# Whole feature takes, four column quarters and one level step fewer in a two-block transformer kernel

## The chip, the cores and the metric

The kernel runs on one core of a Trainium2 chip. The metric is device time in microseconds of one execution. The kernel before was run three times: 1009.45, 1008.4 and 1008.05 us, median 1008.4. A fourth execution was profiled; the rows below come from it.

## The reference, cut to what matters

Two blocks follow each other on 256 tokens of 1024 features, in fp32.

```python
x = first_block(x, ...)       # attention with forget gates, sparse attention, then a 16-expert MoE
return second_block(x, ...)   # two layers:

def hybrid_layer(x, w_in, w_out, g_pre, g_post, lb, g_head, sinks):
    h = rms_norm_2(x, g_pre)
    proj = h @ w_in                                  # [256, 1024] x [1024, 6400]
    q_h, f_h, i_h, z_h, q_a, k_a, v_a, z_a = split(proj)
    o_h = hgrn2(q_h, f_h, i_h, lb)                   # gated recurrence over time, 8 heads of 128
    o_h = rms_norm_2(o_h, g_head) * silu(z_h)
    o_a = sliding_window_attention(rotary(q_a), rotary(k_a), v_a, sinks) * silu(z_a)
    y = concat([o_h, o_a]) @ w_out
    return x + rms_norm_2(y, g_post)
```

In `hgrn2` the query is silu(q_h), the forget gate f and the key 1 - f come from the sigmoid of f_h, and a score between two times is weighted, feature by feature, by the product of the f between them. In block 1 `compress_blocks` multiplies overlapping blocks of 32 tokens by a matrix of 2048 x 256, once for keys and once for values; there are 15 blocks for each of two groups.

## The kernel before, in words

TensorE (PE) multiplies fp32 numbers as fp32r, split in a high and a low part: high x high + high x low + low x high, three products for one (`mm3`, lines 599 to 601). ScalarE (ACT) makes the high part of each 128x512 piece of weights (`w_hi`, line 2027), VectorE (DVE) subtracts it from the raw piece and so makes the low part (`w_lo`, line 454, which is also the line of every other tensor_tensor). Line 457 is that of every tensor_scalar, line 604 that of every transpose by PE.

The work is cut into takes. A take uses two pieces of weights. The order on each engine is written by hand: every engine loops over the takes, feeds the weight pieces up to piece 2t + 9 (four and a half takes ahead), and does at each take what the table `beside` lists for it. A layer of block 2 has 66 takes. Takes 0 to 9 give the attention's q, k and v; takes 10 to 33 are feature takes, whose result has features on partitions and the 256 tokens on columns: za (8), then q, f, q, f (4 each); takes 34 to 49 give i and z of the recurrence by tokens; takes 50 to 65 are the output product. A feature take is 8 times three products of 256 columns (lines 599 to 601, called by `feature_take`); two takes share a PSUM bank, and ACT copies the bank after every second take. Sliding-window attention, eight jobs, runs between the feature takes, two takes apart from take 13 on: scores (line 766), the mask and the maxima on DVE, exponentials on ACT (line 2072), the division on DVE, transposes, `pt_buf` by ACT, values (line 796).

The recurrence is a tree of 8 levels (`level`, lines 1065 to 1087 on PE). At level 0 each time meets itself, at level 1 its neighbour, and so on to halves of 64. Each level is 32 small fp32 products (16 at the last), of 64 rows by 32 columns, which TensorE records as two matmuls each. Between the levels DVE multiplies Q and K by the decays (line 454, gates) and writes the scores through a mask into `buf_c` (line 1809). Levels stand behind takes 35, 37, ... 49. Before level 0, ACT makes sigmoid and silu of f and q (`qf_on`, lines 2102 to 2106), and DVE maps f and 1 - f into their bounds (`qf_bound`).

In block 1 the first matrix of `compress` is applied at takes 33 and 34 (line 820): 16 fp32 products each, of 64 columns of the array (two groups of 32 block slots) by 256 columns, keys to partitions 0 to 63 and values to 64 to 127.

GpSimd (POOL) does small powers, four memsets and the low parts of the experts' rows (line 2468).

Of the kernel before, what the change touches and what calls it, by code (L numbers as in the profile page):

```python
# [30 lines left out]
LEVELS = 8  # L31
AM_DVE, UPPER = 10, 5
# [55 lines left out]
LEVEL_AT = 35  # L88

OUT_L1, OUT_L2, TOK_L1, TOK_L2 = 14, 13, 6, 7  # L90
# [108 lines left out]
def beside_layer(l):  # L199
# [4 lines left out]
    for take, name, i in ((13, "za_on", 0), (20, "za_on", 1), (31, "qf_on", 0), (33, "qf_bound", 0), (33, "qf_on", 1),  # L204
                          (34, "qf_bound", 1), (44, "att_split", 0), (46, "att_split", 1)):
        table.setdefault(b + take, []).append((name, (l, i)))
    for lv in range(LEVELS):
        table.setdefault(b + LEVEL_AT + 2 * lv, []).append(("level", (l, lv)))
# [43 lines left out]
def build(nc, panels, x_in, prm_in, lay_in, pre_in, post_in, head_in, c1_in, c2_in, out):  # L252
    ctx = ExitStack()
    with ctx:
# [90 lines left out]
        blk = [buf_d[:, c * 1024:(c + 1) * 1024].rearrange("p (m g n) -> p m g n", m=16, g=2) for c in range(2)]  # L345
        kc_bd, vc_bd = buf_c[:, 1024:1088], buf_c[0:64, 1088:1216]
        Q, K, FG = gates[:, 0:2048], gates[:, 2048:4096], buf_d[:, :]
# [9 lines left out]
        def sem(name):  # L357
# [6 lines left out]
        w_hi_done = {"act": sem("w_hi_act"), "dve": sem("w_hi_dve")}  # L364
        w_lo_done = {"dve": sem("w_lo_dve"), "pool": sem("w_lo_pool")}
# [11 lines left out]
        forget_x, forget_l, forget, forget_b = (sem("forget_" + n) for n in ("x", "l", "f", "b"))  # L377
        bound_x, bound_e, bounds = sem("bound_x"), sem("bound_e"), sem("bounds")
        route_w, route_hi, route_lo = sem("route_w"), sem("route_hi"), sem("route_lo")
# [6 lines left out]
            sem("cmp_" + n) for n in ("mm", "v", "a", "z", "blk", "ms", "rs", "n", "s", "f"))  # L386
        up_hi, up_lo, mix, mix_hi, mix_lo = (sem(n) for n in ("up_hi", "up_lo", "mix", "mix_hi", "mix_lo"))
# [161 lines left out]

        def turns_of(x, lv):  # L550
            m = 1 << max(lv - 1, 0)
            return x.rearrange("p (b two m) -> p b two m", two=2, m=m)[:, :, 1 if lv else 0, :]
# [44 lines left out]
        def pe_program():  # L597
# [102 lines left out]

            def pair_turns(c, b, src3):
# [38 lines left out]
            def scores(job):  # L740
                pe.wait_ge(score_in, job)
                if job < FOX_JOBS:
                    pe.wait_ge(side, 5)
                    pe.wait_ge(forget_b, 1)
# [55 lines left out]
            def compress(step):  # L800
# [10 lines left out]
                elif step < 5:  # L811
# [6 lines left out]
                    for n in range(8):  # L818
                        for c in range(2):
                            m = T.matmul(ps[c * 64:(c + 1) * 64, 7, 0:256],  # L820
                                         blk[c][:, 8 * h + n, :, :].rearrange("p g n -> p (g n)"),
                                         w1[c][:, n, :], start=h == 0 and n == 0, stop=h == 1 and n == 7)
                elif step == 5:
                    pe.wait_ge(cmp_a, 1)
                    for i in range(2):
                        m = turn128(ps[:, 7, i * P:(i + 1) * P], scr[:, i * P:(i + 1) * P])
# [238 lines left out]
            def level(arg):  # L1065
                l, lv = arg
                b = 2 + lv % 2
                if lv == 0:
# [3 lines left out]
                else:  # L1072
                    pe.wait_ge(level_qk, LEVELS * l + lv)
                    if lv == LEVELS - 1:
                        pe.wait_ge(upper, UPPER * l + 1)
                    elif lv > 1:
                        pe.wait_ge(level_am, AM_DVE * l + 2 * (lv - 1))
                for n in range(NCH):
                    if lv == LEVELS - 1:
# [4 lines left out]
                    for h in range(2):  # L1084
                        c, half = n * P + h * HD, slice(h * HD, (h + 1) * HD)
                        m = T.matmul(ps[half, b, n * 32:(n + 1) * 32], K[:, c:c + HD], turns_of(Q[:, c:c + HD], lv),  # L1086
                                     start=True, stop=True)
                m.then_inc(level_mm, 1)

            def cross(arg):  # L1090
                l, j = arg
                pe.wait_ge(level_qk, LEVELS * (l + 1))
# [87 lines left out]
            for l in range(LAYERS):  # L1180
# [4 lines left out]
                for t in range(t0 + 4, t0 + L_ATT):  # L1185
# [5 lines left out]
                    elif r < L_IH:  # L1191
                        b, f = feature_at(t0 + L_ZA, t)
                        feature_take(t, b, f, 2 + l, uses + 3 + (r - L_ZA) // 4)
                    else:
                        token_take(t, (r - L_IH) % 4, PIECE, 1, 2 + l, uses + 9 + (r - L_IH) // 4)
# [13 lines left out]
        def dve_program():  # L1209
            fed = [0]  # L1210

            def feed(n):
                for p in pieces[fed[0]:n]:
                    if p.hi == "dve":
                        dve.wait_ge(*landed(p.load, p.part))
                        dve.wait_ge(taken, p.free)
                        V.tensor_copy(hi_of(p), raw_of(p)).then_inc(w_hi_done["dve"], 1)
                    if p.lo == "dve":
                        dve.wait_ge(w_hi_done[p.hi], p.hi_count)
                        tt(lo_of(p), raw_of(p), hi_of(p).bitcast(F32), ALU.subtract).then_inc(w_lo_done["dve"], 1)  # L1220
# [84 lines left out]
            def fox_k_(_):  # L1305
# [5 lines left out]
                V.tensor_copy(fsum, ps[:, 7, 0:S]).then_inc(forget_b, 1)  # L1311

            def lower(_):
# [12 lines left out]
                dve.wait_ge(route_hi, 1)  # L1326
                tt(wr3[:, :, 32:52], gw, wr3[:, :, 0:20].bitcast(F32), ALU.subtract).then_inc(route_lo, 1)
                dve.wait_ge(bound_e, 1)
# [144 lines left out]
            def compress(step):  # L1473
# [6 lines left out]
                elif step == 2:  # L1480
                    dve.wait_ge(cmp_v, 2)
                    dve.wait_ge(cmp_z, 2)
                    for c in range(2):
                        pos = prmc(("pos_k", "pos_v")[c])
                        for g in range(2):
# [4 lines left out]
                               ALU.add).then_inc(cmp_blk, 1)  # L1490
                elif step == 5:
                    dve.wait_ge(cmp_mm, 5)
                    V.tensor_copy(scr[:, 512:768], ps[:, 7, 0:256]).then_inc(cmp_v, 1)
# [266 lines left out]
            def qf_bound(arg):  # L1760
                l, j = arg
                dve.wait_ge(bounds, 3)
                for n, (buf, add) in enumerate(((FG, 8), (K, 16))):
                    dve.wait_ge(qf_sig, 6 * l + 4 * j + n + 1)
# [8 lines left out]
            def level(arg):  # L1773
                l, lv = arg
# [922 lines left out]
```

## Time and profile before

| | |
|---|---|
| median of 3 runs | 1008.4 us |
| profiled execution | 1006.5 us |
| its span, first to last instruction | 1004.5 us |
| granted TensorE clock, mean | 0.999 of 2.4 GHz |
| PE / DVE / ACT / POOL busy | 98% / 83% / 67% / 5% |
| HBM, mean | 209 GB/s |

The span is about 2 us shorter than the time of its execution, and that time about 2 us shorter than the median of the runs. "Busy" counts a matmul until its last result leaves the array, so that neighbours overlap; what a product costs is read from the distance between starts, not from its duration.

### The profile page before, as it was taken

How to read it: one execution, taken by the hardware profiler on the slowest of the kernel's cores; microseconds unless marked ns; L12 is line 12 of the kernel's file. 1: busy time of each engine (PE TensorE's matmuls, PEld its weight loads, DVE VectorE, ACT ScalarE, POOL GpSimd, SP SyncE). 2: the span in 40 equal slices, each digit the busy share in tenths (PEclk: the TensorE clock that was granted, in tenths of full speed). 3: DMA queues.
4: the chain of work that ended last, by engine and by line, in shares of the span. 5: the costliest groups of instructions: out<-in, count | busy, mean ns of one | idle time of the engine just before them, and what ended most of it. 6: DMA issues, size and time to landing. Idle time of an engine off the chain costs nothing.

```text
span 1004.5 us, 17322 instructions
## 1 busy us (share of the span) xinstructions
PE 983.4 (98%) x6553; PEld 839.8 (84%) x6553; DVE 834.1 (83%) x1609; ACT 668.3 (67%) x1339; POOL 51.5 (5%) x48
## 2 busy tenths in 40 slices
PE   8999999999999999999999999999999999999997
PEld 6878978987888888888878999888887999978885
DVE  6889867868999999999988777699578977689784
ACT  6475556547889889898865576836446477664552
POOL 1202000002002020020000000000100000000010
PEclk9999999999999999999999999999999999999999
DMA  8543253444999999999945343234454543333421
GB/s 349 217 168 126 88 230 145 147 185 158 384 395 340 403 365 355 411 341 385 388 171 200 146 153 143 88 128 164 147 209 153 183 147 127 127 127 127 169 85 42
DMA packets 32083, 211.34 MB, mean 210 GB/s; under 512 B 3584, under 2 KB 3584, under 8 KB 9216
## 3 DMA queue, kind: packets, MB, share of 16 engines
q1 hardware_dynamic: 30416, 204.22, 53.8%
q10 hardware_dynamic: 1584, 6.00, 1.7%
q8 instruction: 54, 0.88, 0.3%
q14 instruction: 29, 0.24, 0.1%
HBM read 209.16 MB, written 1.05 MB: 209 GB/s over the span
## 4 chain that ended last, share of the span: by engine, by line
PE 88%; DVE 7%; ACT 3%; issue 1%; POOL 1%; DVEq 0%; POOLq 0%; ACTq 0%
PE ps L599 25%; PE ps L601 24%; PE ps L600 23%; PE ps L604 4%; PE ps L1086 3%; PE ps L766 2%; DVE w_lo L454 2%; PE ps L796 2%; PE ps L820 1%; POOL stat L466 1%; PE ps L1140 1%; DVE gates L457 1%; DVE buf_d L457 1%; ACT op_rows L2027 0%; PE ps L1044 0%
## 5 line engine op out<-in xcount | busy, mean ns | idle before, releaser
L454 DVE TENSOR_TENSOR w_lo<-ring,w_hi 128x512 fp32r<-128x512 f32 (+1 forms) x624 | 392.9, 681 | 63.1 <-ACT w_hi L2027 61.0
L2027 ACT ACTIVATE w_hi<-ring 128x512 fp32r<-128x512 f32 (+1 forms) x624 | 354.9, 623 | 116.0 <-PE ps L601 108.6
L599 PE MATMUL ps<-w_hi,op_rows 128*128 128x512 f32 (+2 forms) x784 | 306.7, 391 | 6.3 <-DVE op_rows L1240 2.0
L601 PE MATMUL ps<-w_hi,op_rows 128*128 128x512 f32 (+2 forms) x784 | 300.9, 384 | 0.0
L600 PE MATMUL ps<-w_lo,op_rows 128*128 128x512 f32 (+2 forms) x784 | 300.5, 383 | 0.0
L599 PEld LDWEIGHTS ps<-w_hi,op_rows 128*128 128x128 f32 x784 | 147.3, 188 | 39.6 <-DVE w_lo L454 5.0
L601 PEld LDWEIGHTS ps<-w_hi,op_rows 128*128 128x128 f32 x784 | 147.3, 188 | 29.5
L600 PEld LDWEIGHTS ps<-w_lo,op_rows 128*128 128x128 f32 x784 | 147.5, 188 | 27.0
L599 PE MATMUL ps<-op_rows,w_hi 128*128 128x256 f32 x544 | 158.6, 291 | 0.0
L600 PE MATMUL ps<-op_rows,w_hi 128*128 128x256 f32 x544 | 153.8, 283 | 0.0
L601 PE MATMUL ps<-op_rows,w_lo 128*128 128x256 f32 x544 | 153.8, 283 | 0.0
L599 PEld LDWEIGHTS ps<-op_rows,w_hi 128*128 128x128 f32 x544 | 104.0, 191 | 3.8 <-issue 1.1
L600 PEld LDWEIGHTS ps<-op_rows,w_hi 128*128 128x128 f32 x544 | 104.1, 191 | 0.0
L601 PEld LDWEIGHTS ps<-op_rows,w_lo 128*128 128x128 f32 x544 | 104.0, 191 | 0.0
L2072 ACT ACTIVATE s_buf<-s_buf,stat 128x256 f32<-128x256 f32 (+1 forms) x112 | 49.6, 445 | 61.5 <-DVE stat L457 61.4
L466 POOL TENSOR_TENSOR stat<-stat,minus_half 128x1 f32<-128x1 f32 (+4 forms) x22 | 26.7, 1215 | 751.1 <-DVE stat L460 605.2
L454 DVE TENSOR_TENSOR w_lo<-two_ends,w_hi 128x512 fp32r<-128x512 f32 x64 | 43.5, 733 | 0.5 <-ACT w_hi L2027 0.5
L454 DVE TENSOR_TENSOR w_lo<-keys,w_hi 128x512 fp32r<-128x512 f32 x64 | 41.4, 700 | 0.4
L2027 ACT ACTIVATE w_hi<-two_ends 128x512 fp32r<-128x512 f32 x64 | 38.2, 624 | 4.6 <-PE ps L601 4.5
L2027 ACT ACTIVATE w_hi<-keys 128x512 fp32r<-128x512 f32 x64 | 37.8, 624 | 3.5 <-PE ps L601 3.5
L2027 ACT ACTIVATE zin<-ps 128x512 f32<-128x512 f32 (+2 forms) x32 | 17.7, 566 | 27.2 <-PE ps L1114 14.3
L1086 PEld LDWEIGHTS ps<-gates 128*64 128x64 f32 x896 | 27.3, 138 | 9.1 <-issue 9.1
(264 smaller groups left out, 1179.8 us busy)
## 6 DMA issues: line engine op xcount, KB each, us to landing
ring<-in_panels SPq DMA_DIRECT2D x161, 1024.0 KB, 5.0
keys<-in_panels SPq DMA_DIRECT2D x16, 1024.0 KB, 7.4
two_ends<-in_panels SPq DMA_DIRECT2D x16, 1024.0 KB, 7.7
cst<-in_c ACTq DMA_DIRECT2D x1, 1229.0 KB, 9.1
ring<-in_panels ACTq DMA_DIRECT2D x2, 512.0 KB, 5.8
buf_a<-in_pre ACTq DMA_DIRECT2D x2, 512.0 KB, 6.3
keys<-in_post ACTq DMA_DIRECT2D x2, 512.0 KB, 4.1
out<-head SPq DMA_DIRECT2D x2, 512.0 KB, 2.6
```

The lines of the kernel that those rows point to most:

```text
L454: return V.tensor_tensor(o, a, b, op)
L457: return V.tensor_scalar(o, a, s1, s2, op0, op1) if op1 is not None else V.tensor_scalar(o, a, s1, None, op0)
L466: return G.tensor_tensor(o, o, e.to_broadcast(list(o.shape)), ALU.pow)
L599: T.matmul(o, l[0], r[0], start=start, stop=False)
L600: T.matmul(o, l[0], r[1], start=False, stop=False)
L601: return T.matmul(o, l[1], r[0], start=False, stop=stop)
L604: return T.transpose(o, a, ident[0:n, 0:n])
L766: m = T.matmul(ps[:, 2 + e, lo:lo + n], q(a)[half, :], k[half, 0:n], start=True, stop=plain)
L796: m = T.matmul(value_of(job)[half, kt * P:S], v3[:, kt, cc:cc + HD], pt[:, kt * S:S + kt * P], start=kt == 0, stop=kt == 1)
L1086: m = T.matmul(ps[half, b, n * 32:(n + 1) * 32], K[:, c:c + HD], turns_of(Q[:, c:c + HD], lv), start=True, stop=True)
L2027: return A.activation(o, a, ACT.Copy, scale=scale)
L2072: i = A.activation(sc[:, lo:lo + n], sc[:, lo:lo + n], ACT.Exp, bias=ng_[:, c:c + 1], accum_out=sm[:, c:c + 1])
```

## The change

Six things change in the code.

1. A feature take becomes `whole_take`: for each of 8 feature tiles, one product of the high weights by 512 columns (high rows and low rows at once), and one of the low weights by 256. The halves of the sum lie in the two halves of a bank. Banks 0, 1 and 7 are used in turn; ACT copies the bank to a buffer after every take, GpSimd adds the halves.
2. The takes of f come before those of q. `keep_on` (sigmoids) stands at take 30, `q_on` (silu, written with pairs turned) at takes 32 and 33; the copy of a later take stands behind them on ACT.
3. Levels 1 and 2 become one step: products of 64 columns, 32 for each level. Seven steps stand behind takes 34, 36, 39, 41, 43, 45 and 47.
4. DVE's products of Q with the pairs' decays become `qf_pairs` and `scale_pairs`.
5. The zeroing of `buf_c` goes from DVE (take 4) to GpSimd (behind take 33).
6. `compress`: even and odd positions go to column quarters of 32 (slots of 16), ACT copies the odd half, DVE adds it. The rest (semaphores joined, unused feeding code of GpSimd gone) has no instruction of its own.

```diff
+LEVEL_AT = (34, 36, 39, 41, 43, 45, 47)
+FEATURES, FEATURE_BANKS = 24, (0, 1, 7)
...
+            def whole_take(l, t, i, n, uses):
+                w = weights_of(t)
+                b = FEATURE_BANKS[i % 3]
+                if i > 2:
+                    pe.wait_ge(feature_mid, FEATURES * l + i - 2)
...
+                for k in range(KT):
+                    rows_ready(n, k, 1)
+                    c = k % 4 * P
+                    hi, lo = (x[:, c:c + P] for x in w[k // 4])
+                    if k:
+                        T.matmul(ps[:, b, 0:S], lo, hi3[:, k, :], start=False, stop=False)
+                    m = T.matmul(ps[:, b, :], hi, op_both[:, :, k, :], start=k == 0, stop=k == KT - 1)
+                    if k == 0:
+                        T.matmul(ps[:, b, 0:S], lo, hi3[:, k, :], start=False, stop=False)
+                m.then_inc(taken, 1)
...
+                        if r == L_IH:
+                            pe.wait_ge(feature_mid, FEATURES * (l + 1))
...
+                    elif L_ZA <= r < L_IH:
+                        i = r - L_ZA
                         act.wait_ge(taken, t + 1)
-                        copy((Q if n < 4 else K)[:, c:c + 512], ps[:, b, :]).then_inc(out_free[b], 1)
+                        if i > 3:
+                            act.wait_ge(feature_out, FEATURES * l + i - 3)
+                        copy(feature_tmp(i), ps[:, FEATURE_BANKS[i % 3], :]).then_inc(feature_mid, 1)
...
+            def feature_sum(l, t, i):
+                n = i % 8
+                pool.wait_ge(swa_T, 5 * l + 4)
+                pool.wait_ge(feature_mid, FEATURES * l + i + 1)
+                y = feature_tmp(i)
+                G.tensor_tensor((za, K, q_raw)[i // 8][:, n * S:(n + 1) * S], y[:, 0:S], y[:, S:2 * S],
+                                ALU.add).then_inc(feature_out, 1)
...
+            def q_on(arg):
+                l, j = arg
+                act.wait_ge(feature_out, FEATURES * l + 20 + 4 * j)
+                act.wait_ge(value_mm, L1_JOBS + SWA_PAIRS * (l + 1))
...
+            def scale_pairs(hi):
+                was, now, f4 = (x.rearrange("p (b f) -> p b f", f=4) for x in (q_turned, Q, FG))
+                p2 = pairs_f.rearrange("p (b two) -> p b two", two=2)
+                dv(tt(now[:, :, 2 * hi], was[:, :, hi], f4[:, :, 2 * hi], ALU.mult))
+                dv(tt(now[:, :, 2 * hi + 1], was[:, :, 2 + hi], p2[:, :, hi], ALU.mult))
...
+                        if step == 1:
+                            m = T.matmul(ps[half, 2 + n // 8, n % 8 * HD:(n % 8 + 1) * HD], K[:, c:c + HD],
+                                         q_two[:, :, c:c + HD].rearrange("p y (b f) -> p y b f", f=4)[:, :, :, 2:4],
+                                         start=True, stop=True)
...
+                    for n in range(4):
+                        for q in range(4):
+                            odd, c = divmod(q, 2)
+                            m = T.matmul(ps[q * 32:(q + 1) * 32, 7, 0:256],
+                                         blk[c][:, 8 * h + 2 * n + odd, :, :].rearrange("p g n -> p (g n)"),
+                                         w1[c][:, 2 * n + odd, :], start=h == 0 and n == 0, stop=h == 1 and n == 3)
```

PE at the end of the feature takes of a layer, before: the last feature tile of take 33 and the first weight piece of take 34 (`op_rows` are the rows of the layer's input, high or low).

```order
L599 MATMUL ps<-op_rows,w_hi 128x256
L600 MATMUL ps<-op_rows,w_hi 128x256
L601 MATMUL ps<-op_rows,w_lo 128x256
L599 MATMUL ps<-w_hi,op_rows 128x512
L600 MATMUL ps<-w_lo,op_rows 128x512
L601 MATMUL ps<-w_hi,op_rows 128x512
```

The same place now.

```order
L729 MATMUL ps<-op_rows,w_lo 128x256
L730 MATMUL ps<-op_rows,w_hi 128x512
L613 MATMUL ps<-w_hi,op_rows 128x512
L614 MATMUL ps<-w_lo,op_rows 128x512
L615 MATMUL ps<-w_hi,op_rows 128x512
```

A feature tile of three products of 256 columns has become one of 256 and one of 512. The token takes (lines 613 to 615) are as before, but the first of them now stands behind a wait for the copy of take 33.

ACT before, from the weights of take 30 on: `pt_buf` are the copies of the last two attention jobs, `gates<-ps` the copies of takes 31 and 33, `buf_d` and `gates<-gates` sigmoid and silu.

```order
L2027 ACTIVATE pt_buf<-ps 128x768
L2027 ACTIVATE w_hi<-ring 128x512 x2
L2027 ACTIVATE pt_buf<-ps 128x768
L2027 ACTIVATE gates<-ps 128x512
L2103 ACT_TABLE_LOAD
L2103 ACTIVATE buf_d<-gates 128x1024
L2104 ACTIVATE gates<-gates 128x1024
L2106 ACT_TABLE_LOAD
L2106 ACTIVATE gates<-gates 128x1024
L2027 ACTIVATE w_hi<-ring 128x512 x4
L2027 ACTIVATE gates<-ps 128x512
```

ACT now, from the copy of take 30 (`buf_c<-ps`) to the table load before silu.

```order
L2094 ACTIVATE buf_c<-ps 128x512
L2165 ACT_TABLE_LOAD
L2165 ACTIVATE buf_d<-gates 128x1024
L2166 ACTIVATE gates<-gates 128x1024
L2165 ACTIVATE buf_d<-gates 128x1024
L2166 ACTIVATE gates<-gates 128x1024
L2094 ACTIVATE w_hi<-ring 128x512 x2
L2094 ACTIVATE pt_buf<-ps 128x768
L2094 ACTIVATE buf_c<-ps 128x512
L2094 ACTIVATE w_hi<-ring 128x512 x2
L2094 ACTIVATE buf_c<-ps 128x512
L2173 ACT_TABLE_LOAD
```

ACT now, the rows that follow; the last `buf_c<-ps` is the copy of take 33, for which PE waits before take 34.

```order
L2173 ACTIVATE q_two<-gates 128x256x2x2
L2094 ACTIVATE w_hi<-ring 128x512 x2
L2094 ACTIVATE buf_c<-ps 128x512
L2173 ACTIVATE q_two<-gates 128x256x2x2
L2094 ACTIVATE w_hi<-ring 128x512 x8
```

All four sigmoids now stand ahead of three copies, and one table load is gone from the stretch.

DVE before, from the weights of loop 35 to the masks of level 2; `gates<-gates,buf_d` is the product of Q or K with the decays, COPY_PREDICATED a level's masks.

```order
L454 TENSOR_TENSOR w_lo<-ring,w_hi 128x512 x4
L454 TENSOR_TENSOR gates<-gates,buf_d 128x1024
L1809 COPY_PREDICATED buf_c<-cst,ps 64x16x32 x2
L454 TENSOR_TENSOR w_lo<-ring,w_hi 128x512 x4
L454 TENSOR_TENSOR buf_d<-buf_d 128x1024
L454 TENSOR_TENSOR gates<-gates,buf_d 128x2048
L1809 COPY_PREDICATED buf_c<-cst,ps 64x16x32 x2
L454 TENSOR_TENSOR w_lo<-ring,w_hi 128x512 x4
L454 TENSOR_TENSOR gates<-gates,buf_d 128x512x2 x2
L454 TENSOR_TENSOR buf_b<-buf_d 128x512
L1809 COPY_PREDICATED buf_c<-cst,ps 64x16x16x2 x2
```

DVE now, from the second half of `scale_pairs` to the masks of steps 0 and 1 and the weights behind them.

```order
L462 TENSOR_TENSOR q_two<-q_two,buf_d 128x512
L462 TENSOR_TENSOR q_two<-q_two,pt_buf 128x512
L1843 COPY_PREDICATED buf_c<-cst,ps 64x16x32 x2
L462 TENSOR_TENSOR w_lo<-ring,w_hi 128x512 x4
L462 TENSOR_TENSOR q_two<-q_two,pt_buf 128x512x2
L462 TENSOR_TENSOR gates<-gates,pt_buf 128x512x2
L462 TENSOR_TENSOR buf_b<-pt_buf 128x512
L1843 COPY_PREDICATED buf_c<-cst,ps 64x16x32 x2
L1843 COPY_PREDICATED buf_c<-cst,ps 64x16x16x2 x2
L462 TENSOR_TENSOR w_lo<-ring,w_hi 128x512 x6
```

Four masks, those of levels 1 and 2, now stand in one piece ahead of the weights, where two masks stood between each two takes' weights; `qf_pairs` (a 128x1024 product to `pt_buf`) and the first half of `scale_pairs` stand ahead of this piece.

## Rows read from the trace of the kernel before

**Rows 1.** Part 1 of the page: busy time, share, instructions.

```profile
PE 983.4 (98%) x6553; PEld 839.8 (84%) x6553; DVE 834.1 (83%) x1609; ACT 668.3 (67%) x1339; POOL 51.5 (5%) x48
```

**Rows 2.** Waits of PE: total us, times, longest us.

```profile
PE ps L1086 <- DVE gates L457: 4.0, 2, 2.0
```

**Rows 3.** Timeline of PE: start us, duration; products of 512, then 256 columns.

```profile
535.73 0.39 PE L601 MATMUL ps<-w_hi,op_rows 128*128 128x512 f32 x1
...
545.93 0.39 PE L601 MATMUL ps<-w_hi,op_rows 128*128 128x512 f32 x1
...
547.27 0.28 PE L601 MATMUL ps<-w_hi,op_rows 128*128 128x256 f32 x1
...
550.15 0.28 PE L601 MATMUL ps<-w_hi,op_rows 128*128 128x256 f32 x1
```

**Rows 4.** Chain that ended last: start us, us on the chain.

```profile
668.50 0.43 PE ps L599
...
697.10 1.99 PE ps L1086 x64
...
704.75 1.08 PE ps L1081 x32
...
785.42 0.87 PE ps L604 x8
```

**Rows 5.** Timeline of PE: the compress product.

```profile
144.02 3.67 PE L820 MATMUL ps<-ring,buf_d 128*64 128x256 f32 x32
```

**Rows 6.** Timeline of PE, layer 0: behind take 30, and start of take 33.

```profile
631.25 0.87 PE L796 MATMUL ps<-pt_buf,zin 128*64 128x256 f32 x8
...
640.06 0.39 PE L599 MATMUL ps<-op_rows,w_hi 128*128 128x256 f32 x1
```

**Rows 7.** Timeline of ACT, layer 0, takes 30 to 33.

```profile
630.68 0.80 ACT L2027 ACTIVATE pt_buf<-ps 128x768 f32<-128x768 f32 x1
...
635.84 0.60 ACT L2027 ACTIVATE gates<-ps 128x512 f32<-128x512 f32 x1 [2.06 <-PE ps L601]
636.46 1.28 ACT L2103 ACT_TABLE_LOAD   x1
637.75 1.06 ACT L2103 ACTIVATE buf_d<-gates 128x1024 f32<-128x1024 f32 x1
638.72 1.04 ACT L2104 ACTIVATE gates<-gates 128x1024 f32<-128x1024 f32 x1
...
642.03 2.19 ACT L2027 ACTIVATE w_hi<-ring 128x512 fp32r<-128x512 f32 x4
```

**Rows 8.** Timeline of POOL: beside an almost idle DVE, then a busy one.

```profile
242.37 0.74 POOL L2468 TENSOR_TENSOR op_rows<-gates,op_rows 128x256 fp32r<-128x256 f32 x1 [1.81 <-ACT op_rows L2027]
...
302.12 3.60 POOL L2468 TENSOR_TENSOR op_rows<-gates,op_rows 128x256 fp32r<-128x256 f32 x2 [57.39 <-ACT op_rows L2027]
```

**Rows 9.** Timeline of DVE: without, then beside POOL's two adds after 306 us.

```profile
298.86 2.49 DVE L454 TENSOR_TENSOR w_lo<-ring,w_hi 128x512 fp32r<-128x512 f32 x4
...
306.20 3.59 DVE L454 TENSOR_TENSOR w_lo<-two_ends,w_hi 128x512 fp32r<-128x512 f32 x4
```

**Rows 10.** Timeline of DVE, layer 0, bounds and levels.

```profile
647.68 0.74 DVE L454 TENSOR_TENSOR zin<-ps,scr 128x256 f32<-128x256 f32 x2
648.35 1.37 DVE L457 TENSOR_SCALAR buf_d<-buf_d,lay 128x256 f32<-128x256 f32 x4
...
664.50 2.67 DVE L1809 COPY_PREDICATED buf_c<-cst,ps 64x512 f32<-64x512 uint32 x2
...
669.62 2.36 DVE L454 TENSOR_TENSOR gates<-gates,buf_d 128x1024 f32<-128x1024 f32 x2
671.89 1.08 DVE L454 TENSOR_TENSOR buf_b<-buf_d 128x512 f32<-128x512 f32 x1
```

**Rows 11.** Busy time by stage: attention, levels (PE, PEld, DVE, ACT, POOL; clock, DMA, GB/s).

```profile
580.00:610.00 30.00, 30.00 (x257) 27.99 (x255) 23.08 (x58) 22.30 (x54) 0.00 (x0) 1.00 0.41 153
651.20:705.00 53.80, 53.80 (x626) 44.90 (x628) 50.55 (x64) 26.15 (x48) 0.00 (x0) 1.00 0.41 147
```

**Rows 12.** Line of the attention's scores: durations ns, first and last start.

```profile
L766 PE MATMUL ps<-keys,zin x64: 269/324/480, 565.5 to 624.5; 64*128 64x256 f32 x32, 64*128 64x128 f32 x32
```

More of the change, by code:

```diff
@@ L203, in beside_layer @@
     at_takes(table, [(j0 + i, tuple(b + take for take in takes)) for i, takes in enumerate(ATT_2)])
-    for take, name, i in ((13, "za_on", 0), (20, "za_on", 1), (31, "qf_on", 0), (33, "qf_bound", 0), (33, "qf_on", 1),
-                          (34, "qf_bound", 1), (44, "att_split", 0), (46, "att_split", 1)):
+    for take, name, i in ((13, "za_on", 0), (20, "za_on", 1), (30, "keep_on", 0), (30, "keep_on", 1), (32, "q_on", 0), (33, "q_on", 1),
+                          (32, "qf_bound", 0), (33, "qf_bound", 1), (34, "qf_pairs", 0), (44, "att_split", 0), (46, "att_split", 1)):
         table.setdefault(b + take, []).append((name, (l, i)))
-    for lv in range(LEVELS):
-        table.setdefault(b + LEVEL_AT + 2 * lv, []).append(("level", (l, lv)))
+    for step, take in enumerate(LEVEL_AT):
+        table.setdefault(b + take, []).append(("level", (l, step)))
     for j in range(2):
@@ L548, in k_of, with feature_tmp, bank_of @@
             return K[:, j * 1024:(j + 1) * 1024]
+        def feature_tmp(i):
+            return buf_c[:, i % 4 * 512:(i % 4 + 1) * 512]
+        def bank_of(step):
+            return 7 if step in (0, 2) else 2 + (step + 1) % 2
         def turns_of(x, lv):
@@ new lines, in level @@
+            def level(arg):
+                l, step = arg
+                lv = step + 1
+                if step == 0:
+                    f2, k2 = (x.rearrange("p (b two) -> p b two", two=2) for x in (FG, K))
+                    dve.wait_ge(qf_sig, 6 * (l + 1))
+                    settle()
+                    scale_pairs(1)
+                    dve.wait_ge(level_mm, STEPS * l + 1)
+                    settle()
+                    tt(k2[:, :, 0], k2[:, :, 0], f2[:, :, 1], ALU.mult).then_inc(level_qk, 1)
+                    scale_pairs(0)
+                    dve.wait_ge(am_zero, l + 1)
+                    take_masked(l, 0, ps[:, bank_of(0), :].rearrange("p (n x) -> p n x", n=NCH), 0)
+                    return
+                dve.wait_ge(level_mm, STEPS * l + step + 1)
+                m = 1 << step
+                tot = pairs_f if step == 1 else buf_b[:, slice(*totals[lv - 1])]
+                qv, kv = (x.rearrange("p (b two m) -> p b two m", two=2, m=m) for x in (Q, K))
+                tv = tot.rearrange("p (b two) -> p b two", two=2)
+                dve.wait_ge(level_qk, STEPS * l + step)
+                settle()
+                tt(qv[:, :, 1, :], qv[:, :, 1, :], bc(tv[:, :, 0], m), ALU.mult)
+                last = tt(kv[:, :, 0, :], kv[:, :, 0, :], bc(tv[:, :, 1], m), ALU.mult)
+                if step + 1 < STEPS:
+                    last = tt(buf_b[:, slice(*totals[lv])], tv[:, :, 0], tv[:, :, 1], ALU.mult)
+                last.then_inc(level_qk, 1)
+                if step == 1:
+                    both = ps[:, 2:4, :].rearrange("p a (n y x) -> p (a n) y x", y=2, x=32)
+                    take_masked(l, 1, both[:, :, 0, :], 2)
+                    take_masked(l, 2, both[:, :, 1, :], 4)
+                elif step < 4:
+                    take_masked(l, lv, ps[:, bank_of(step), :].rearrange("p (n x) -> p n x", n=NCH), 2 * lv)
@@ L1911, in behind @@
                 for name, arg in beside.get(t, ()):
-                    if name in table and name not in ("log_in", "weigh", "scores_out", "qf_bound", "up_split"):
+                    if name in table and name not in ("log_in", "weigh", "scores_out", "qf_bound", "qf_pairs", "up_split"):
                         table[name](arg)
@@ L1992, in dve_program @@
                     ahead(t)
-                    if r == 4:
-                        V.memset(buf_c[:, :], 0.0).then_inc(am_zero, 1)
                     behind(t)
```

227 lines of the change are left out of this document (101 added, 126 removed).

## The prediction

> **What bounds the kernel now.** I read the busy times first. The reader is to see PE busy for 98% of the span and DVE, the next, for 83% [rows 1]. Next come PE's waits: of all that compete, one line concerns the edited stages, level 0's first product waiting for DVE's bound gates, 4.0 us in two waits, one a layer [rows 2]. So in these stages PE sets the pace, and a shorter PE program is a shorter kernel, unless another engine is late instead. How near the others are is read in busy time by stage: in 30 us of attention DVE is busy for 23.08 and ACT for 22.30, in the levels DVE is busy for 50.55 of 53.8 [rows 11]. The attention stage has room for new work on DVE and ACT; the level stage has almost none on DVE. Last I read PE's timeline for prices by spacing, since durations overlap: a run of 512-column products goes from 535.73 to 545.93 in 45 steps, 0.2267 each, one of 256-column products from 547.27 to 550.15 in 24 steps, 0.12 each [rows 3].
>
> **Feature takes.** A feature tile goes from three products of 256 columns (3 x 0.12 = 0.36) to one of 512 and one of 256 (0.2267 + 0.12 = 0.3467). Eight tiles a take: 2.88 becomes 2.77, 0.107 saved. With 24 takes and two layers, 48 x 0.107 = 5.1 us, 2.55 a layer. What is saved is the fixed part of a product; the columns streamed are the same.
>
> **Levels.** One step of 32 products goes: 1.99 on the chain, and the restart of the 512-column products behind it, where the first stands 0.43 on the chain instead of 0.23, so 0.2 [rows 3, 4]. The merged step has 64-column products; 64 records of 32 columns take 1.99, 32 records of 64 columns 1.08 [rows 4], so I put it at 2.15 for 1.99. Net -2.05 a layer.
>
> **Compress.** The 32 records of 256 columns come in 3.67 us, 0.115 each [rows 5]. A single fp32 stream would need more: transposes of 128 columns take 0.87/8 = 0.109 each [rows 4], about twice that for a record of 256. So the two column halves run beside each other. If four quarters do the same, each of the two multiplications halves; 3.67 includes some 0.2 of the last record's own end, so 2 x 3.45/2 = -3.45; if only two run at a time, nothing. I take the first, since a quarter differs from a half by the same division of columns and the halves show no loss. The Trainium skill (TensorEngine Tiling (Array Packing), Tiling Modes) lists 128x32 as four independent tiles, which would give the -3.45; no row here shows four. The added ACT copy and DVE add of the odd half stand one take ahead of the use, in a stage where PE alone is full; I cost them at nothing, and uncovered they would cost about 1 us each time, by a 0.60 copy [rows 7] and 0.74 for two sums of 256 columns [rows 10].
>
> **The new wait before take 34.** Level 0's wait goes: 2.0. PE now waits before take 34 for ACT's copy of take 33. Take t = 0 at 631.25, the values product behind take 30. Take 33 began 8.81 later [rows 6]; two shorter takes make it 8.6, and its end 11.4. ACT in its new order, each step at its pitch (about 0.1 under the duration; the sigmoids follow each other by 0.97) [rows 7]: 0.2 until the bank is full, copy 0.6, table 1.3, four sigmoids 3.9, two high parts 1.05, `pt_buf` 0.7, copy 0.5, two high parts 1.05, copy 0.5, table 1.3, silu 1.0, two high parts 1.05, copy of take 33 0.6: 13.75. PE waits 2.4. Queued behind that copy on ACT are the second silu and the high parts of later takes, which are four takes ahead and not late. POOL's add (0.74 alone [rows 8]) and the last silu end at 15.7, behind a take 34 that runs from 13.8 to 16.5, so level 0 itself is not late. Nothing is bound on SP: the weights' transfers are issued from there as before. The zeroing of `buf_c` stands behind the last add on POOL and before the first mask, near 24.
>
> **DVE in the level stretch.** ACT's last sigmoid ends at 6.0; behind it and the low parts due by then DVE works without a pause from about 7.7, an estimate: three values of 0.35, sixteen bounds 5.2, two pairs of low parts 2.4, `qf_pairs` 1.2 (17.55), a pair of low parts 1.2, `scale_pairs` 2 x 1.08, K 1.2 (22.1), `scale_pairs` 2.15, masks 2.65 (27.0), four low parts 2.5 (29.5), step 1's products 2.35 and 0.7 (32.5), four masks 5.3 (37.9), and the first low part that take 40 needs, 0.6: 38.5 [rows 9, 10]. PE: 16.5, level 0 2.0, two takes 5.65 (24.1), step 1 2.15, three takes 8.35 (34.65), step 2 2.0, restart 0.2: take 40 could begin at 36.9. It waits 1.7, and step 3 then 0.3. Behind DVE's masks stand the low parts of all later takes, hence PE. `scale_pairs` has no row of its own. With 16-byte steps it is nearest to the 1.08 for 512 strided columns [rows 10]; at the price of a plain product (2.36 for two of 1024, so some 0.65 for 512 with its start) it saves 4 x 0.4 = 1.6 a layer.
>
> **POOL beside DVE.** Four low parts take 2.49 us on DVE alone and 3.59 beside two of POOL's adds [rows 9], so an add costs DVE 0.55 at most; over the other adds it came to less, and I take 0.37. Three fall into the DVE chain above: 1.1 a layer. In the attention stage a job comes with every two takes: eight jobs' scores start from 565.5 to 624.5 [rows 12], so a pair of takes with its job lasts some (59.0 - 0.7)/7 = 8.3, the 0.7 for the eighth job's own records. DVE has 23.08/30 of that busy [rows 11], 6.4; two adds make 7.1 to 7.5 of the new 8.1 (8.3 less twice 0.107), and ACT's one more copy of 0.60 [rows 7] makes 22.30/30 x 8.3 + 0.6 = 6.8: both still fit. The Trainium skill (SBUF — State Buffer, SBUF: two separate sides) says that a GpSimd operation that reads SBUF and a VectorE operation with two SBUF inputs shut each other out for a whole instruction. By that, an add would cost DVE its full 0.74 and the chain 1.1 a layer more, 2.2 in all; the 0.55 above is under it, and the 3.60 for two adds [rows 8] shows the shutting out in the other direction.
>
> **The sum.** A layer: -2.55 - 2.05 - 2.0 + 2.4 + 1.7 + 0.3 + 1.1 = -1.1; two layers -2.2; compress -3.45; together -5.65. The profiled execution of before took 1006.5 (its span 1004.5), so 1000.9; it stood 1.9 under the median of the runs, so against that median of 1008.4 the forecast is 1002.8.
>
> **Rivals.**
> Four quarters do not run beside each other (the trace shows two): 3.45 lost, 1006.2. For it: no row shows four streams. Against it: the halves lose nothing.
> DVE is not late in the level stretch: `scale_pairs` at 0.65 and adds that cost nothing give 2.65 a layer back, 997.5. For it: the 17.55 and the 38.5 sum many small terms. Against it: DVE is already at 94% there [rows 11].
> Slower: POOL's adds stop DVE for longer. Between takes 13 and 30 DVE has 8.1 - 6.4 = 1.7 spare for each pair of takes, so it decides from 0.85 an add on; at 1.3 an add DVE overruns by 0.9 a pair, 8 pairs a layer, 14.4 in both layers: 1017; at 1.1, 0.5 a pair, 8.0 and 1011. For it: POOL's own add grew from 0.74 to 1.8 beside a busy DVE [rows 8], so the two do get in each other's way. Against it: 0.55 in the row that shows DVE.
> The whole takes save nothing, if a 512-column product between 256-column ones costs more than 0.2267 by the 0.0133 that a tile saves: 1007.9.
>
> **How the numbers follow.** Chances: forecast 0.45, with its own range 1000 to 1005.5; quarters by halves 0.25; DVE in time 0.12; POOL's adds 0.08; no gain by whole takes, or a wait at take 34 or in the levels that is larger by some 2 us a layer, 0.10. A measurement of this kernel can tell about 0.2%, 2 us, from no change: faster is under 1006.4, slower over 1010.4. Faster: 0.45 + 0.12 + a little over half of 0.25 + some of the last, 0.74. Same: the rest of the quarters and most of the last, 0.16. Slower: 0.10. The range from 996 (DVE in time, and a little less) to 1008.5 (the quarters and a larger wait together) leaves out the POOL rival and the tails.
>
> **What would show it.** Right: feature tiles every 0.347 us; PE waiting twice for ACT's copy, about 2.4 each, and no more for the bounds; PE waiting for a DVE low part near take 40, 1.7 to 3; the compress line twice at 1.9 in place of 3.67; POOL's adds at 0.75 to 1.8 with PE's waits in the attention stage no larger than before. Wrong: a compress line that still takes 3.67; PE idle before feature takes 13 to 30; a wait of level 0 for `scale_pairs` or POOL's last add; a merged step of over 3 us.

## The result: 1017.2 us, slower by 0.9%

The changed kernel took 1017.2 us (four runs, 1016.7 to 1018.0) against 1008.35 of before: a ratio of 1.0087, interval 1.0072 to 1.0102. Its profiled execution has a span of 1016.2 us, 11.7 more than before; the medians differ by 8.9, since the profiled execution of before lies 1.8 under its median and that of the changed kernel 0.7 over. The page's busy times and its line of granted clock, in tenths for 40 slices of the span, of the changed kernel:

```profile
PE 981.9 (97%) x6041; PEld 817.7 (80%) x6041; DVE 850.6 (84%) x1614; ACT 674.4 (66%) x1360; POOL 96.2 (9%) x98
PEclk9999999999999999999999999989999999998999
```

Beside [rows 1] PE has 512 products fewer and is busy for hardly less: some of the others ran at a slower clock. PE's waits in the changed kernel (total us, times, longest), those that answer to [rows 2] and the new ones:

```profile
PE ps L613 <- DVE w_lo L462: 8.4, 6, 3.1
PE ps L830 <- DVE zin L462: 6.1, 4, 2.0
...
PE ps L613 <- ACT buf_c L2094: 2.0, 2, 1.0
...
PE ps L1134 <- DVE gates L465: 1.6, 2, 0.8
```

Level 0's wait fell from 2.0 to 0.8 a layer, but values now wait for DVE (L830, 3.0 a layer), and take 40 for a low part (3.1). All of PE's waits together went from 14.6 to 27.7. The products in the next rows cost about what was forecast. Timeline of the changed kernel's PE (start, duration): the second compress product, a feature take, and the two long waits of layer 0.

```profile
142.60 1.93 PE L855 MATMUL ps<-ring,buf_d 128*32 128x256 f32 x32
144.46 0.39 PE L613 MATMUL ps<-op_rows,w_hi 128*128 128x256 f32 x1
...
597.88 0.28 PE L729 MATMUL ps<-op_rows,w_lo 128*128 128x256 f32 x1
...
599.61 0.28 PE L729 MATMUL ps<-op_rows,w_lo 128*128 128x256 f32 x1
...
605.65 0.87 PE L830 MATMUL ps<-pt_buf,zin 128*64 128x256 f32 x8 [1.98 <-DVE zin L462]
...
656.83 2.10 PE L1126 MATMUL ps<-q_two,gates 128*64 128x64 f32 x64
...
672.83 0.77 PE L613 MATMUL ps<-w_hi,op_rows 128*128 128x512 f32 x1 [3.10 <-DVE w_lo L462]
```

The compress product has a row of 1.93 where it was 3.67 [rows 5], and 1.86 pass to the next start; five feature tiles take 1.73, 0.346 each; the merged step takes 2.10. At each of the two waits the clock falls. Busy time by stretch of the changed kernel (PE, PEld, DVE, ACT, POOL; then clock):

```profile
606.00:610.00 4.00, 4.00 (x23) 3.14 (x20) 3.84 (x9) 3.79 (x8) 1.72 (x2) 0.60 0.10 18
...
672.00:678.00 6.00, 5.17 (x12) 4.13 (x13) 6.00 (x9) 0.00 (x0) 0.00 (x0) 0.50 0.47 169
```

0.50 is the lower of the clock's two levels, 1.2 of 2.4 GHz. In layer 0 it stands from 606.8 for 3.4 us, which is 1.2 us after the end of the first wait, and from 671.7 for 6.8 us, of which the first 1.1 still lie in the second wait; layer 1 has the same two stretches. That is 20.5 us at half the clock, a loss of 10.2 us, or 9.1 without the part in which PE waited anyway. So the difference of the spans, 11.7, adds up to within a microsecond: -11.2 for products (4.1 for the levels and 3.45 for compress as forecast, and 3.7 instead of 5.1 for the feature takes, which is worked out in the part on the prediction), +13.1 for waits, +9.1 to +10.2 for the clock.

Where the waits come from is read on DVE and POOL. First the attention stage before: PE begins a job's scores; DVE divides for the job ahead of it, makes two low parts and takes the scores out of PSUM.

```profile
599.06 0.92 PE L766 MATMUL ps<-keys,zin 64*128 64x256 f32 x8
```

```profile
597.92 1.01 DVE L457 TENSOR_SCALAR s_buf<-s_buf,stat 128x128 f32<-128x128 f32 x4
598.84 1.29 DVE L454 TENSOR_TENSOR w_lo<-ring,w_hi 128x512 fp32r<-128x512 f32 x2
600.05 0.95 DVE L454 TENSOR_TENSOR s_buf<-ps,cst 128x768 f32<-128x768 f32 x1
```

The changed kernel in layer 0, PE's scores of the same job and then DVE: the wait for ACT at the silu of za, the softmax's division, the low parts and the scores ahead of the late values, then the bounds, the masks and the low parts ahead of take 40.

```profile
596.22 0.92 PE L800 MATMUL ps<-keys,zin 64*128 64x256 f32 x8
```

```profile
596.81 1.30 DVE L462 TENSOR_TENSOR w_lo<-ring,w_hi 128x512 fp32r<-128x512 f32 x2 [3.87 <-ACT w_hi L2094]
...
598.43 1.50 DVE L465 TENSOR_SCALAR s_buf<-s_buf,stat 128x128 f32<-128x128 f32 x4
599.85 1.83 DVE L462 TENSOR_TENSOR w_lo<-ring,w_hi 128x512 fp32r<-128x512 f32 x2
601.60 0.94 DVE L462 TENSOR_TENSOR s_buf<-ps,cst 128x768 f32<-128x768 f32 x1
...
605.18 0.42 DVE L462 TENSOR_TENSOR zin<-ps,scr 128x256 f32<-128x256 f32 x1
...
644.37 1.37 DVE L465 TENSOR_SCALAR buf_d<-buf_d,lay 128x256 f32<-128x256 f32 x4
645.66 3.36 DVE L465 TENSOR_SCALAR gates<-gates,lay 128x256 f32<-128x256 f32 x4
...
666.64 5.31 DVE L1843 COPY_PREDICATED buf_c<-cst,ps 64x512 f32<-64x512 uint32 x4
671.99 3.70 DVE L462 TENSOR_TENSOR w_lo<-ring,w_hi 128x512 fp32r<-128x512 f32 x6
```

POOL of the changed kernel at those times:

```profile
598.56 0.76 POOL L2532 TENSOR_TENSOR gates<-buf_c 128x256 f32<-128x256 f32 x1 [3.86 <-ACT buf_c L2094]
600.09 1.04 POOL L2532 TENSOR_TENSOR gates<-buf_c 128x256 f32<-128x256 f32 x1 [0.77 <-ACT buf_c L2094]
...
646.39 1.84 POOL L2580 MEMSET buf_c<- 128x2048 f32 x1
```

Beside one add, four divisions take 1.50 and two low parts 1.83, where the same took 1.01 and 1.29 without: 0.5 an add. So DVE falls behind PE: before, it takes a job's scores 1.0 to 2.0 us after PE has begun them, in all eight jobs of the layer; now the second to fifth job are taken 3.9, 4.1, 3.6 and 5.4 us after (the last is 596.22 to 601.60 above), and then PE waits for the values. Further on, four bounds take 3.36 where four take 1.37, 2.0 lost: POOL's zeroing stands beside them, and its last add beside their start (e1 parts the two). Behind that stand four masks, 5.31, and only then the low part that take 40 needs.

### The profile page after: what moved, and what is told of

Read it like the earlier page. It is cut to its first block, busy times and chain, and to the rows that moved or that the text cites. A ratio compares the mean times of both kernels' runs of the same rounds, so it can differ in the third digit from the quotient of the medians.

```text
span 1016.2 us, 16393 instructions
## 1 busy us (share of the span) xinstructions
PE 981.9 (97%) x6041; PEld 817.7 (80%) x6041; DVE 850.6 (84%) x1614; ACT 674.4 (66%) x1360; POOL 96.2 (9%) x98
## 4 chain that ended last, share of the span: by engine, by line
PE 71%; DVE 17%; ACT 6%; issue 3%; DMA 2%; POOL 1%; SPq 0%; DVEq 0%; ACTq 0%; POOLq 0%
PE ps L613 19%; PE ps L615 18%; PE ps L614 18%; DVE w_lo L462 5%; PE ps L618 3%; PE ps L730 3%; DMA ring<-in_panels 2%; ACT s_buf L2138 2%; DVE s_buf L465 1%; PE ps L800 1%; PE ps L729 1%; DVE buf_c L1843 1%; PE ps L1134 1%; PE ps L830 1%; DVE q_two L462 1%
## 5 line engine op out<-in xcount | busy, mean ns | idle before, releaser
L730 PE MATMUL ps<-op_rows,w_hi 128*128 128x512 f32 x384 | 142.4, 408 | 0.0
L729 PE MATMUL ps<-op_rows,w_lo 128*128 128x256 f32 x336 | 94.6, 282 | 0.0
L730 PEld LDWEIGHTS ps<-op_rows,w_hi 128*128 128x128 f32 x384 | 72.5, 190 | 15.4 <-issue 0.8
L729 PEld LDWEIGHTS ps<-op_rows,w_lo 128*128 128x128 f32 x336 | 64.3, 191 | 2.2
L2094 ACT ACTIVATE buf_c<-ps 128x512 f32<-128x512 f32 (+3 forms) x64 | 35.7, 557 | 26.5 <-PE ps L730 11.9
L613 PE MATMUL ps<-op_rows,w_hi 128*128 128x256 f32 x160 | 46.6, 291 | 0.0
L614 PE MATMUL ps<-op_rows,w_hi 128*128 128x256 f32 x160 | 45.2, 283 | 0.0
L615 PE MATMUL ps<-op_rows,w_lo 128*128 128x256 f32 x160 | 45.2, 283 | 0.0
```

What stands on the lines that cost most here:

```text
L613: T.matmul(o, l[0], r[0], start=start, stop=False)
L614: T.matmul(o, l[0], r[1], start=False, stop=False)
L615: return T.matmul(o, l[1], r[0], start=False, stop=stop)
L729: T.matmul(ps[:, b, 0:S], lo, hi3[:, k, :], start=False, stop=False)
L730: m = T.matmul(ps[:, b, :], hi, op_both[:, :, k, :], start=k == 0, stop=k == KT - 1)
L2094: return A.activation(o, a, ACT.Copy, scale=scale)
```

## The experiments

Two theories. **Order**: the waits come from where three things stand (the zeroing beside the bounds, the values behind masks and low parts, level 2's masks ahead of low parts), and the clock follows the waits. **Load**: POOL's adds and the new work overload DVE, and an edit of the order only moves the wait. Each kernel was timed in 5 rounds beside the kernel before (1008.5).

**e1**, the zeroing later:

```diff
                             pool.wait_ge(feature_out, FEATURES * (l + 1))
+                            pool.wait_ge(qf_ready, 2 * (l + 1))
                             G.memset(buf_c[:, :], 0.0).then_inc(am_zero, 1)
```

> The changed kernel, but GpSimd's zeroing of buf_c waits for DVE's last bounds (qf_ready), so that it runs beside two-input products instead of beside tensor_scalar. Order theory: the 3.36 us of the last four bounds fall to 1.4, level 0 waits 0 instead of 0.8, the wait near take 40 falls from 3.1 to about 1.9 in each layer; 2.0 us a layer at least, 4.5 if the clock behind it no longer falls: 1013 to 1008. Load theory (DVE is simply overloaded by GpSimd's work): the zeroing holds up whatever it stands beside, DVE is as late as before, 1016 to 1018.

1012.5 (ratio 1.0035, 1.0022 to 1.0048), 4.7 less. DVE, then POOL, of e1:

```profile
644.45 1.80 DVE L465 TENSOR_SCALAR gates<-gates,lay 128x256 f32<-128x256 f32 x4
646.17 1.28 DVE L462 TENSOR_TENSOR w_lo<-ring,w_hi 128x512 fp32r<-128x512 f32 x2
```

```profile
646.37 1.81 POOL L2581 MEMSET buf_c<- 128x2048 f32 x1 [1.24 <-DVE gates L465]
```

The bounds are down to 1.80, since an add stands beside them still; so of the 2.0 lost, 1.6 was the zeroing and 0.4 the add. The zeroing costs the two-input low parts nothing. Level 0 waits no more, and the time is in the order theory's range; but take 40 still waits 2.8 and not 1.9, since PE, without its wait at level 0, comes earlier too.

**e2**, values out of PSUM ahead of masks and low parts in two loops:

```diff
+            early = [T_L2 + L2_TAKES * l + take for l in range(LAYERS) for take in (23, 31)]
...
-                    if name in ("log_in", "weigh", "scores_out", "qf_bound", "qf_pairs"):
+                    if name in ("log_in", "weigh", "scores_out", "qf_bound", "qf_pairs") or name == "values_out" and t in early:
...
```

> The changed kernel, but in loops 23 and 31 of a layer DVE multiplies the values out of PSUM ahead of the scores' mask and of the weights' low parts. Order theory: PE's wait of 2.0 before the values of job 2, and the stretch of 3.2 us at clock 0.5 behind it, go, 3.6 us at that place; since ACT's chain of softmax steps is then what is late, a part comes back before take 34: 1010 to 1014. Load theory (DVE too full beside GpSimd's adds): another wait of about 2 us stands in the attention stage: 1016 to 1018. Product-mix theory of the clock: the clock still falls to 0.5 near 607 us though nothing waits.

1014.6 (1.0062, 1.0048 to 1.0075), 2.6 less, just over the range that the order theory gave. The wait of 2.0 and the slower clock at 607 are gone with the products unchanged, which speaks against the product-mix theory (e3 kept this wait and had no slower clock there, so this place alone doesn't settle it; e5, with the same products, does: its six executions have mean clocks of 0.997 to 0.999, the four of the changed kernel 0.988 to 0.990). But new waits of 1.07 (the next values) and 0.81, and 2.0 instead of 1.0 before take 34, with a new stretch of 3.4 us at clock 0.5 behind that one in layer 0, give half back, as the load theory has it.

**e3**, level 2's masks behind step 2's products:

```diff
-                    take_masked(l, 2, both[:, :, 1, :], 4)
                 elif step < 4:
+                    if step == 2:
+                        both = ps[:, 2:4, :].rearrange("p a (n y x) -> p (a n) y x", y=2, x=32)
+                        take_masked(l, 2, both[:, :, 1, :], 4)
```

> The changed kernel, but DVE's two masks of level 2 stand behind step 2's products instead of ahead of the low parts of loops 37 to 39. Order theory: the wait of 3.1 before take 40 falls to about 0.4, and the 6.7 us at clock 0.5 behind it go: 5 to 5.6 us a layer, less up to 1 for step 3: 1006.5 to 1009. Load theory: step 3 then waits for its products by 2 to 3 us instead: 1012 to 1017. Product-mix theory of the clock: the clock falls at 671 us all the same, 1011.

1012.8 (1.0042, 1.0021 to 1.0063), a miss for the order theory and in the load theory's range, with the wait before step 3 that it named. Its cause, though, is another that I hadn't seen: step 3 writes the bank that these masks read, and e5, where it writes another, doesn't have the wait. The eight executions of e3 took 1009.5 to 1018.3, at mean clocks of 0.999 to 0.988. PE's waits of e3 in block 2:

```profile
PE ps L1134 <- DVE buf_c L1843: 5.1, 2, 2.6
```

**e4**, the three together: 

> The three edits together. Order theory: what is left of the new waits is about 1 to 3 us a layer before take 34, clock near 0.999: by the sum of products saved (2 x 4.6 and 3.4) and the old waits, 996 to 1001. Load theory: 1010 or more.

1007.5 (0.9994, 0.9985 to 1.0003): between the two theories.

**e5**, three more edits of order:

```diff
-            return 7 if step in (0, 2) else 2 + (step + 1) % 2
+            return 7 if step in (0, 2) else 4 if step == 3 else 2 + (step + 1) % 2
...
-                            pe.wait_ge(feature_mid, FEATURES * (l + 1))
+                            pe.wait_ge(feature_mid, FEATURES * (l + 1) - 1)
...
-for take in (23, 31)]
+for take in (23, 25, 31)]
```

> The version with the three edits, and three more: step 3 writes PSUM bank 4, so that it doesn't wait for level 2's masks to leave bank 2; PE waits before take 34 for the copy of take 32 only (bank 7 of take 33 is not written before step 2); values out early in loop 25 too. Order theory: the waits of 2.4 before step 3 and 2.05 before take 34 go, two a layer, with what the clock lost behind the first: 1007.5 - 4.8 - 3.3 - 1.5 = 998, between 996 and 1001. Load theory: DVE and ACT are late anyway, the waits turn up at level 0 and at low parts: 1003 to 1008.

1005.9 (0.9970, 0.9958 to 0.9982), a miss of 8 us for the order theory and in the load theory's range. (Step 0 writes bank 7 ahead of step 2, but it stands behind the silu that needs take 33's copy.) The two waits went, and PE waits elsewhere (waits of e5 in block 2, as are those of the kernels below):

```profile
PE ps L618 <- ACT pt_buf L2100: 3.4, 4, 1.3
PE ps L1134 <- DVE gates L465: 2.6, 2, 1.3
PE ps L1134 <- DVE buf_b L462: 2.4, 2, 1.2
...
PE ps L830 <- DVE zin L462: 1.7, 2, 0.9
```

**e6**, e5 with two 256-column products for the one of 512 in 7 of 8 tiles:

```diff
+                    if k:
+                        T.matmul(ps[:, b, 0:S], hi, hi3[:, k, :], start=False, stop=False)
+                        m = T.matmul(ps[:, b, S:2 * S], hi, lo3[:, k, :], start=False, stop=k == KT - 1)
+                        continue
...
```

> The same kernel, but for 7 of 8 feature tiles the 512-column product (high weights by both rows) is two products of 256 columns. If PE sets the pace there and whole takes save 0.0133 a tile, as the prediction had it: 7/8 of 5.1 = 4.5 us more than the version before, about 1002. If the saving is lost in waits all the same (the takes are not what bounds the attention stage): within 1 us of the version before.

1006.6 (0.9981, 0.9972 to 0.9989), 0.7 more than e5, which is within the spread of the runs. From start to start, without waits, the feature takes of block 2 take 143.0 us in e6's trace and 140.2 in e5's: 2.8 was added and not 4.5. PE's waits in block 2 fell by 1.8 (12.9 to 11.1) in return: PE no longer sets the pace alone in that stage.

**e7**, the changed kernel without the adds (ACT copies the high half straight to its place; here and in e9 and e11 GpSimd copies one column a take, so that the order stays):

> The changed kernel without GpSimd's adds: ACT copies the 256 columns of the high rows' half to their place itself, and the low rows' half of the sum is left out. If the adds are what made the waits in the attention stage (load theory): the wait of 2.0 before job 2's values falls under 0.5, no clock loss behind it, 3.5 us a layer, 1009 to 1011. If they are but one part (order theory): 1.0 to 1.5 of the 2.0 goes, for two adds of 0.5 and a copy shorter by 0.2; the wait before take 40 stays at 2 to 3, time 1010 to 1014.

1005.6 (0.9966, 0.9953 to 0.9979): 11.6 less, more than either theory gave. PE's waits of e7:

```profile
PE ps L613 <- DVE w_lo L462: 6.9, 3, 3.1
PE ps L613 <- ACT gates L2094: 1.6, 2, 0.8
PE ps L830 <- DVE zin L462: 1.3, 2, 0.7
```

The attention stage's waits fell from 6.1 to 1.3; the order in the level stage is untouched, and its wait stays.

**e8**, e5 with the feature takes of before:

```diff
-                    m = T.matmul(ps[:, b, :], hi, op_both[:, :, k, :], start=k == 0, stop=k == KT - 1)
+                    m = mm3(ps[:, b, i % 2 * S:(i % 2 + 1) * S], tuple(x[:, c:c + P] for x in w[k // 4]),
+                            (hi3[:, k, :], lo3[:, k, :]), k == 0, k == KT - 1)
...
```

> The version with all six edits, but with the feature takes of the kernel before: three products of 256 columns, two takes in a bank (banks 0, 1, 7 in turn), one ACT copy of 512 columns for two takes, and no add by GpSimd. Products cost 5.1 more than in the version before. Load theory (the ACT copies and GpSimd's adds cost ACT and DVE more than PE saves): the waits of the attention stage go and those at the levels shrink, together over 8 us of 12.9: below 1003, 998 to 1002. If the order alone mattered: 5 us slower than e5, 1011.

998.1 (0.9898, 0.9882 to 0.9913): faster than both kernels, with the whole takes given up. All waits of PE in block 2 of e8:

```profile
PE ps L1130 <- DVE buf_b L462: 2.4, 2, 1.2
PE ps L613 <- DVE op_rows L462: 1.0, 1, 1.0
PE ps L613 <- DVE w_lo L462: 0.7, 1, 0.7
```

**e9** and **e11** part the adds from the copies; both leave out the sum of the halves, e9 with copies of 256 columns, e11 of 512.

> The version with all six edits and whole takes, without GpSimd's adds: ACT copies the high rows' half itself, the low rows' half of the sum is left out. If adds and copies are what is left: waits of the attention stage near 0, level stage about 2 us, 996 to 999. If DVE and ACT are late without them too: 1002 to 1005.

> As e9 (all six edits, whole takes, no adds by GpSimd), but ACT's copy after each take has its full 512 columns again; the sums are left out. Add theory: it is GpSimd's adds beside DVE that cost the 10 us between e5 (1005.9) and e9 (995.7): within 2.5 us of e9, 996 to 998. Copy theory: it is ACT's longer copies, 48 x 0.2 us: 1003 to 1006.

e9 took 995.7 (0.9878, 0.9861 to 0.9896), e11 996.3 (0.9887, 0.9872 to 0.9903). Between e5 and e11 only the adds differ, with what waits for their results: 9.6 us for 48 adds. In e11 DVE takes every job's scores of layer 0 within 2.3 us, where e5 has up to 5.7. The longer copies cost 0.6 at most, which is within the spread of the runs. PE's wait that e11 has and e8 hasn't is that for silu at level 0:

```profile
PE ps L1134 <- ACT q_two L2179: 1.6, 2, 0.8
```

**e10**, e8 with the old compress: 

> As e8, with the compress step of the kernel before (two column halves). If the quarters run beside each other and nothing else bounds there: 3.4 us more than e8. If the gain is given back by a later stage: within 1 us of e8.

1002.0 (0.9936, 0.9922 to 0.9950), 3.9 more than e8: the quarters are worth what was forecast.

**e12**, the add on DVE:

```diff
+                        dve.wait_ge(feature_mid, FEATURES * l + i + 1)
+                        tt((za, K, q_raw)[i // 8][:, i % 8 * S:(i % 8 + 1) * S], ps[:, FEATURE_BANKS[i % 3], 0:S],
+                           feature_tmp(i)[:, 0:S], ALU.add).then_inc(feature_out, 1)
...
```

> As e5 (all six edits, whole takes), but ACT copies only the low rows' half (256 columns) and DVE adds it to the half in PSUM, 0.42 us a take, while GpSimd adds nothing. Add theory (an add by GpSimd costs DVE about as much as the add itself, 0.5, and comes at bad times): at or below e5, 998 to 1004. If DVE has no room for 24 x 0.42 a layer: waits for DVE grow, 1006 to 1012.

1013.0 (1.0047, 1.0032 to 1.0061), worse than e5 by 7, and just over the range of its slower theory. DVE of e12, then PE's largest wait:

```profile
593.87 0.42 DVE L462 TENSOR_TENSOR gates<-ps,buf_c 128x256 f32<-128x256 f32 x1 [0.77 <-ACT buf_c L2106]
...
606.54 0.43 DVE L462 TENSOR_TENSOR gates<-ps,buf_c 128x256 f32<-128x256 f32 x1 [1.10 <-ACT buf_c L2106]
```

```profile
PE ps L1134 <- ACT q_two L2185: 5.7, 2, 2.9
```

The add takes 0.42, but DVE stands still before it until ACT has copied, and the softmax behind it stands too. The silu of q, for which level 0 waits, now stands behind these adds as well, and a bank is free for PE only after DVE's add.

**e13**, the changed kernel with the old takes alone: 

> The changed kernel with the feature takes of the kernel before alone (pairs of takes in a bank, one copy by ACT for two, no adds), and none of the six edits but the shorter wait before take 34 that goes with it. If whole takes with copies and adds are the larger part of the loss: the attention stage has no new waits, the wait before take 40 stays near 3 with its slower clock: 1003 to 1007. If the level stage is the larger part: 1010 or more.

1010.3 (1.0018, 1.0007 to 1.0029), 6.9 less than the changed kernel, where the second of the two ranges begins. PE's waits of e13:

```profile
PE ps L613 <- DVE w_lo L462: 7.0, 4, 3.1
PE ps L1130 <- DVE gates L465: 1.7, 2, 0.8
```

From e13 to e8 the edits of order give 12.2, most of it in the level stage, since e13 has no long wait in the attention stage. So the loss has two parts, and neither theory alone has it: whole takes with their adds made the kernel 7 to 8 us slower (e13 under the changed kernel, e8 under e5), and the order of the zeroing, the masks and the bank, with the early values, some 11 to 12.

## Why the prediction was wrong

The forecast was 1002.8, with a range up to 1008.5; measured were 1017.2. The profiled span is 17.3 us longer than the forecast has it (1004.5 - 5.65): 6.1 by waits (13.1 more than before, for 7.0 forecast), 9.1 to 10.2 by the clock, 1.4 by the feature takes.

Right, by their own rows: a tile within a feature take (0.346 for 0.3467), the merged step (2.10 for 2.15), compress (e10). Take 34 began where it was worked out, 13.9 us after the values of take 30 for 13.8, though its wait was 1.0 and not 2.4, since the values' wait had already made PE late; in e2 and e4, without that wait, it was 2.0. The wait at level 0 was to go and fell from 2.0 to 0.8. The wait before take 40 came out as 3.1 for 1.7 + 0.3 + 1.1 = 3.1, and that is luck: DVE's low part was done 41.2 us after the values of take 30, for 38.5 + 1.1, 1.6 late by the zeroing; PE stood there at 38.25 for 36.9, 0.8 of it by level 0's wait. The three adds beside this chain cost 1.35 for 1.1.

The feature takes saved 3.7 and not 5.1. PE at the start of two takes and at the first product behind them, of e8, then of e11:

```profile
590.77 0.36 PE L613 MATMUL ps<-op_rows,w_hi 128*128 128x256 f32 x1
...
596.69 0.87 PE L826 MATMUL ps<-pt_buf,zin 128*64 128x256 f32 x8
```

```profile
589.70 0.47 PE L730 MATMUL ps<-op_rows,w_hi 128*128 128x512 f32 x1
...
595.44 0.87 PE L830 MATMUL ps<-pt_buf,zin 128*64 128x256 f32 x8
```

Two takes last 5.92 and 5.74, 0.09 a take for 0.107. Over all 48, from start to start and without waits, they last 143.2 us in e8, as before, and 139.5 in e11. The price of a tile was read in the middle of a run; at the start of a take the next product begins 0.31 to 0.34 after the one of 512 columns, not 0.2267, where it begins 0.12 to 0.20 after the one of 256 in e8. With the wait for silu this accounts for e11's gain over e8: 3.7 - 1.6 = 2.1, for 1.8 measured.

Wrong, and larger, were three terms.

"In the attention stage ... both still fit." The step compared busy time with the period: 7.1 to 7.5 of 8.1. What counted was the softmax's chain over both engines: DVE's maxima, ACT's exponentials, DVE's division, and the values behind them. At the silu of za, with its two table loads, the chain stands still on ACT (DVE waits 3.87 there, 3.39 before), and it catches up only with what a period leaves over. An add costs 0.5 where DVE is on that chain (1.50 for 1.01), which is near the row that was shown; the mistake was to price it at nothing there. e11 shows the price: 9.6 us for 48 adds, against 3.7 saved by PE. The forecast's slower rival named the adds, but asked for more than 0.85 an add; 0.5 was enough. That its figure for 1.3 an add, 1017, is the time measured is chance: no add cost that, and the zeroing, the masks and the clock, which that rival has not, made the rest. The Trainium skill (SBUF — State Buffer, SBUF: two separate sides) has a GpSimd operation and certain VectorE operations shut each other out for a whole instruction; the direction agrees, with 0.5 lost for adds of 0.76 to 1.04.

The zeroing on POOL has no term in the sum. It took 1.6 of DVE's time a layer (3.36 in the changed kernel, 1.80 in e1), for 1.84 of its own. By the same section of the Trainium skill a GpSimd operation that reads nothing from SBUF does not stop a VectorE operation that only has two SBUF inputs. e1 agrees: 1.28 for two low parts beside the zeroing. The move is worth 4.7 us to the kernel.

The clock had no term. The prediction priced a wait by its length. Two waits of 2 to 3 us a layer, 10.2 in all, came with another 9.1 to 10.2 us, as much as the waits themselves.

What stays open is what lets the clock fall at one wait and not at another like it.

## What to carry to other kernels

A stage with room in each engine's busy time may have none in a chain that goes back and forth between two engines: add new work to the chain's period, at the step where it is latest, before counting it as hidden. Work moved to GpSimd is not off VectorE's path; look at which VectorE instructions run beside it. A wait of PE can cost more than its length: here the two long ones cost about twice that. A saving on PE is worth only what the late engines leave of it: 0.7 of 2.8 us between e6 and e5.

## What the runs showed of the hardware

In the changed kernel the clock fell to 0.50 after a wait of 1.98 and within one of 3.10 us, and stayed there for some 3.4 and 6.8 us. The length of a wait doesn't decide it: before, a wait of 2.0 at level 0 left the clock at 1.00 [rows 2, 11], and in e3 waits of 1.96 and 2.57 in layer 0 did too, while that of 2.57 in layer 1 did not. Short waits were followed by a fall as well: 1.2 before step 3, with step 3's small products behind it, in e8 and e10 in layer 0 and in e5 in layer 1, and 1.74 in block 1 of e13; e7 and e13 have one near 229 us, in block 1, where the longest wait of PE close by was 0.5. The executions of one kernel differ too, as those of e3 show. Busy time of e8:

```profile
682.00:684.00 2.00, 2.00 (x6) 1.52 (x6) 2.00 (x3) 1.96 (x5) 0.00 (x0) 0.50 0.81 213
```

Four column quarters of 128x32 run beside each other: 32 records of 256 columns in 1.86 us to the next start, 0.058 each, half of the 0.115 for halves (3.67 for 32) [rows 5]. That is the four independent tiles of the Trainium skill (TensorEngine Tiling (Array Packing), Tiling Modes).
